# Column sums of the modulation products by one-column matmuls, and a shorter stage ahead of the first block, in a two-block transformer kernel

## The reference

```
mod = (silu(c) @ ada_w[l] + ada_b[l]).reshape(B, 3, 3, 1024)   # first block: 9 groups of 1024
h = rms_norm(x, norm_g[l, 0]) * (1 + scale) + shift
x = x + 0.5 * gate * swiglu(h, ffn1_w_in[l], ffn1_w_out[l])
ada = c_2 @ w_ada_2[l] + b_ada_2[l]                            # second block: 6 groups of 1024 per layer
```

## Time and profile before

| | us |
|---|---|
| median of 3 runs | 3195.17 |
| lowest, highest | 3194.53, 3200.88 |
| the profiled execution | 3195.94 |
| its span, first to last instruction | 3194.3 |
| TensorE, VectorE, ScalarE busy | 2939.4 (92%), 2336.1 (73%), 1363.4 (43%) |
| GpSimd busy | 186.3 (6%) |
| read from HBM | 545.29 MB, 171 GB/s over the span |
| mean granted TensorE clock | 0.956 of full |

### The profile page before, as it was taken

The page is one execution under the profiler, slowest core; times in us unless marked ns, Lnnn a source line. Parts: engine busy times, 40 slices in busy tenths (PEclk is TensorE's granted clock), DMA queues, the critical chain, the costliest instruction groups (busy, mean ns, idle before and its releaser), DMA issues.

```text
span 3194.3 us, 61745 instructions
## 1 busy us (share of the span) xinstructions
PE 2939.4 (92%) x22464; PEld 2718.6 (85%) x22464; DVE 2336.1 (73%) x3735; ACT 1363.4 (43%) x1973; POOL 186.3 (6%) x204
## 2 busy tenths in 40 slices
PE   3998997979989879999999999999799999999998
PEld 2998994969989778999998878898799899988787
DVE  6776933447778766997888986656449978899765
ACT  1434541224344524554444445445345544444444
POOL 1011000301101101011000000000000200000000
PEclk7999986989999989999999999999899999999999
DMA  7785530027867656444444545544345454445454
GB/s 274 273 276 169 180 133 14 1 92 245 276 211 282 199 178 224 159 163 159 163 158 152 165 156 191 195 153 137 102 154 175 152 165 158 160 156 170 159 194 140
DMA packets 149586, 547.98 MB, mean 172 GB/s; under 512 B 16609, under 2 KB 16737, under 8 KB 149089
## 3 DMA queue, kind: packets, MB, share of 16 engines
q1 hardware_dynamic: 124704, 454.29, 42.3%
q0 software_dynamic: 24336, 89.14, 8.4%
q10 hardware_dynamic: 432, 2.97, 0.2%
HBM read 545.29 MB, written 1.05 MB: 171 GB/s over the span
## 4 chain that ended last, share of the span: by engine, by line
PE 65%; DVE 11%; ACT 2%; issue 1%; DVEq 0%; ACTq 0%; POOL 0%; POOLq 0%
PE acc L1962 15%; PE st L1512 10%; PE st L1508 10%; PE st L1509 9%; PE acc L1968 7%; DVE w_lo L752 4%; PE st L1933 3%; PE acc L1508 2%; PE acc L1509 2%; PE acc L1512 2%; ACT w_hi L395 1%; DVE arena L1214 1%; PE st L1555 1%; PE acc L1891 1%; DVE arena L808 1%
## 5 line engine op out<-in xcount | busy, mean ns | idle before, releaser
L752 DVE TENSOR_TENSOR w_lo<-ring,w_hi 128x1024 fp32r<-128x1024 f32 x864 | 1087.3, 1260 | 553.1 <-ACT w_hi L395 545.8
L395 ACT ACTIVATE w_hi<-ring 128x1024 fp32r<-128x1024 f32 x864 | 910.6, 1054 | 1007.4 <-PE st L1512 821.0
L1508 PE MATMUL st<-h_hi,w_hi 128*128 128x256 f32 x3952 | 989.3, 288 | 6.1 <-ACT arena L681 3.5
L1509 PE MATMUL st<-h_lo,w_hi 128*128 128x256 f32 x3952 | 970.7, 283 | 0.0
L1508 PEld LDWEIGHTS st<-h_hi,w_hi 128*128 128x128 f32 x3952 | 758.2, 192 | 18.3 <-issue 9.7
L1509 PEld LDWEIGHTS st<-h_lo,w_hi 128*128 128x128 f32 x3952 | 759.2, 192 | 1.0
L1512 PE MATMUL st<-h_hi,w_lo 128*128 128x256 f32 x3952 | 559.1, 284 | 22.2 <-DVE w_lo L752 21.5
L1512 PEld LDWEIGHTS st<-h_hi,w_lo 128*128 128x128 f32 x3952 | 510.1, 192 | 29.8 <-DVE w_lo L752 29.6
L1962 PE MATMUL acc<-w_hi,act_hi 128*128 128x512 f32 x1016 | 322.5, 399 | 3.9 <-DVE act_lo L1326 3.9
L1962 PE MATMUL acc<-w_hi,act_lo 128*128 128x512 f32 x1016 | 316.0, 392 | 0.0
L714 ACT ACTIVATE act_hi<-arena 128x256 fp32r (+1 forms) x256 | 106.6, 418 | 409.4 <-PE acc L1968 401.2
(11 more groups left out here) (286 smaller groups left out, 3279.6 us busy)
## 6 DMA issues: line engine op xcount, KB each, us to landing
ring<-weights SPq DMA_DIRECT2D x864, 512.0 KB, 3.3
arena<-ada_weights POOLq DMA_DIRECT2D x168, 512.0 KB, 5.2
arena<-const ACTq DMA_DIRECT2D x1, 2112.0 KB, 8.7
x_t<-params SPq DMA_DIRECT2D x1, 1024.0 KB, 8.7
out<-arena POOLq DMA_DIRECT2D x1, 1024.0 KB, 4.2
k<-const ACTq DMA_DIRECT2D x1, 473.0 KB, 4.8
arena<-smallw ACTq DMA_DIRECT2D x1, 320.0 KB, 10.4
par<-params SPq DMA_DIRECT2D x1, 198.5 KB, 4.6
```

Source lines behind the costliest of these rows:

```text
L395: nc_a.activation(w_hi[:, u % 2, :], ring[:, u % RING, :], ACT.Copy).then_inc(hi_ready, 1)
L752: v.tensor_tensor(w_lo[:, u % 2, :], ring[:, u % RING, :], w_hi[:, u % 2, :], ALU.subtract)\
L1508: mm(dst(t), w, hi_t(t), start=start, stop=False, skip_group_check=True)
L1509: mm(dst(t), w, lo_t(t), start=False, stop=False, skip_group_check=True)
```

## The change

1. `piece` and `total` become `columns`: each of the eight 128x128 tiles of the summed buffer is the stationary operand, and one column of ones streams through it. The sums come out as a 128x8 column block in PSUM, in 8 matmuls per block.
2. `take` becomes one addition of the bias, PSUM to `mod` (128x8). The product with the identity, the reduction, `take_block`, `add_bias` and the buffer `diag` go.
3. `Q_FFN = (2, 8)`: only blocks 0 and 1 (shift and scale) are done in the stage "ada". Block 2 (the gate) moves into bodies 0 and 1 of the first feed-forward, block 3 into bodies 2 to 4: 4, 4, 3, 3, 2 macs. Before it was 0, 2, 2, 2, 2 (the second feed-forward keeps that).
4. `part_ffn` shrinks to two buffers; the first mac of a block in the loop waits until TensorE has read the buffer (`ada_piece`).
5. Transfers: x is issued when modulation unit 7 has landed, ring units 0 and 1 at unit 11, ring units 2 and 3 at unit 15.
6. ACT loads the silu table at once and squares x ahead of rounding units 0 and 1; DVE takes the reciprocal of the norm inside the stage, ahead of the stage's end.

```diff
@@ constants
-Q_FFN = (3, 8)
+Q_FFN = (2, 8)
+EARLY_MACS = (4, 4, 3, 3, 2)
+FIRST_IN_LOOP = (3, 8)
...
-        part_ffn = ar(4 * T, 5, UNIT)
+        part_ffn = ar(4 * T, 2, UNIT)
@@ SP
-            sp.wait_ge(ada_landed[1], 16)
+            sp.wait_ge(ada_landed[3], 32)
             sp.dma_start(x_t[:, :, :].rearrange("p a t -> p (a t)"), params[:, N_PAR:N_PAR + DT * T])\
               .then_inc(sem("x_in"), 16)
             for s in range(RING):
+                if s == 0:
+                    sp.wait_ge(ada_landed[3], 48)
+                elif s == 2:
+                    sp.wait_ge(ada_landed[3], 64)
                 sp.dma_start(ring[:, s, :], weights[s]).then_inc(landed[s], 16)
@@ ACT
+            eng.wait_ge(sem("zrow"), 1)
+            nc_a.activation(spare[:, :], spare[:, :], ACT.Silu)
             eng.wait_ge(sem("par_in"), 16)
             eng.wait_ge(sem("k1_in"), 16)
             nc_a.activation(sc[:, :], pc("c"), ACT.Silu).then_inc(sem("silu_c"), 1)
+            eng.wait_ge(sem("x_in"), 16)
+            squares(0)
             hi(U_FFN1)
             hi(U_FFN1 + 1)
-            eng.wait_ge(sem("x_in"), 16)
-            squares(0)
             stage(eng, ST["ada"])
@@ DVE
-            def take(q, r, src, i=None, upto=None, between=None):
...
-                v.tensor_tensor(diag, src.rearrange("p (u n) -> p u n", n=P),
-                                ident.unsqueeze(1).to_broadcast([P, 2, P]), ALU.mult).then_inc(ada_diag, 1)
...
-                v.tensor_reduce(dst, diag, AX, ALU.add).then_inc(sem("ada_mod"), 1)
...
+            def take(q, bank, i=None):
+                eng.wait_ge(ada_piece, plus(i, 1, q + 1))
...
+                v.tensor_tensor(dst, bank, bias, ALU.add).then_inc(sem("ada_mod"), 1)
...
                 for k in range(8):
                     mac(q, k, part[:, q % 2, :])
                     if k == 3 and q > 0:
-                        take_block(q - 1, st[:, 2 * ((q - 1) % 2):, :])
+                        take(q - 1, st[:, q - 1, 0:8])
+            eng.wait_ge(sem("x_in"), 16)
+            eng.wait_ge(sem("std"), 1)
+            link(v.reciprocal(rstd, std))
             lo(U_FFN1)
+            take(1, st[:, 1, 0:8])
+            taken_blocks(Q_FFN[0])
+            scale1_of(0)
             lo(U_FFN1 + 1)
-            take_block(Q_FFN[0] - 1, st[:, 2 * ((Q_FFN[0] - 1) % 2):, :])
-            add_bias(0, Q_FFN[0])
-            scale1_of(0)
...
                 def body(j, i=None, per=0):
                     t, k = max(j - 1, 0) // 4, (j - 1) % 4
+                    def macs(half):
+                        if j > 4:
+                            if (k, half) == (0, 0):
+                                eng.wait_ge(ada_piece, plus(i, 1, q0 + t))
+                            mac(q0 + t, 2 * k + half, part_ffn[:, 0, :], i)
+                        else:
+                            mine = early[j]
+                            for q, m in (mine[:len(mine) // 2], mine[len(mine) // 2:])[half]:
+                                mac(q, m, part_ffn[:, 1 if q < q0 else 0, :])
                     step(base + 2 + 3 * j, i, per)
+                    macs(0)
                     step(base + 3 + 3 * j, i, per)
                     mult(j + 1, i)
+                    if f == 0 and j == 4:
+                        take(q0 - 1, st[:, 2 + (j + 1) % 2, T:T + 8])
+                    if j > 4 and k == 0:
+                        take(q0 + t - 1, st[:, 2 + (j + 1) % 2, T:T + 8], i)
+                    macs(1)
+                    lower(j + 1, i)
+                    step(base + 4 + 3 * j, i, per)
...
-                take_block(q0 + 4, st[:, 2:4, :])
-                add_bias(q0, q0 + 5)
+                take(q0 + 4, st[:, 2, T:T + 8])
+                taken_blocks(q0 + 5)
@@ PE
-            def piece(q, r, dst, sums, i=None):
-                mm(dst, ones, sums, start=True, stop=True, skip_group_check=True).then_inc(ada_piece, 1)
...
+            def columns(q, dst, sums, i=None):
+                eng.wait_ge(ada_taken, plus(i, 8, 8 * q + 8))
+                for m in range(8):
+                    ins = mm(dst[:, m:m + 1], sums[:, m * P:(m + 1) * P], ones[:, 0:1], start=True, stop=True,
+                             skip_group_check=True)
+                ins.then_inc(ada_piece, 1)
...
-            for q in range(Q_FFN[0]):
-                total(q, st[:, 2 * (q % 2):, :], reused=q >= 2)
+            columns(0, st[:, 0, 0:8], part[:, 0, :])
             eng.wait_ge(sem("zrow"), 1)
             squares(0)
+            columns(1, st[:, 1, 0:8], part[:, 1, :])
             stage(eng, ST["ada"])
...
                 def body(j, i=None, per=0):
+                    if f == 0 and j == 4:
+                        columns(q0 - 1, st[:, 2 + (j + 1) % 2, T:T + 8], part_ffn[:, 1, :])
+                    if j > 4 and (j - 1) % 4 == 0:
+                        columns(q0 + (j - 1) // 4 - 1, st[:, 2 + (j + 1) % 2, T:T + 8], part_ffn[:, 0, :], i)
...
```

More of the change, by code:

```diff
@@ L121, with early_macs @@
 EXTRA = 3328
+FIRST_IN_LOOP = (3, 8)
+def early_macs(f):
+    if f == 0:
+        steps, counts = [(q, m) for q in (2, 3) for m in range(8)], EARLY_MACS
+    else:
+        steps, counts = [(Q_FFN[1], m) for m in range(8)], (0, 2, 2, 2, 2)
+    ends = [sum(counts[:j + 1]) for j in range(5)]
+    return [steps[e - c:e] for e, c in zip(ends, counts)]
 def build(nc, weights, ada_weights, params, const1, const2, smallw, out):
@@ L746, in _ @@
             v = nc.vector
+            v.memset(spare[:, :], 0.0)
             v.memset(zrow[:, :], 0.0).then_inc(sem("zrow"), 1)
@@ L810, in mac, with taken_blocks @@
                 ins.then_inc(ada_taken, 1)
[L812 to L835 removed]
+            def take(q, bank, i=None):
+                eng.wait_ge(ada_piece, plus(i, 1, q + 1))
+                at = _COLS["ada_b"][0] + 8 * q
+                dst, bias = (mod[:, 8 * q:8 * q + 8], par[:, at:at + 8]) if i is None else \
+                    (mod[:, bass.ds(i * 8 + 8 * q, 8)], par[:, bass.ds(i * 8 + at, 8)])
+                v.tensor_tensor(dst, bank, bias, ALU.add).then_inc(sem("ada_mod"), 1)
+            def taken_blocks(n):
+                eng.wait_ge(sem("ada_mod"), n)
             def scale1_of(s):
@@ L1146, in _ @@
                 if l == 0:
-                    take_block(Q_PROJ + 2, st[:, 0:2, :])
+                    take(Q_PROJ + 2, st[:, 0, 0:8])
                 for m in range(2):
@@ L1163, in out_steps @@
                             if k in OUT_TAKES:
-                                q = OUT_TAKES[k]
-                                take_block(q, banks[:, 2 * (q % 2):, :])
+                                take(OUT_TAKES[k], banks[:, 3, 0:8])
                 out_steps(0, 4)
@@ L1621, in ffn @@
                 eng.wait_ge(sem("act_lo"), FT * f + FT)
-                for r in range(4):
-                    piece(q0 + 4, r, quarter(st[:, 2:4, :], r), part_ffn[:, 4, r * T:(r + 1) * T])
+                columns(q0 + 4, st[:, 2, T:T + 8], part_ffn[:, 0, :])
                 b = (FT - 1) % 2
@@ L1860, in _ @@
                     eng.wait_ge(sem("smax"), AH)
-                    total(Q_PROJ + 2, st[:, 0:2, :])
+                    columns(Q_PROJ + 2, st[:, 0, 0:8], part[:, (Q_PROJ + 2) % 2, :])
                 stage(eng, ST[f"attn{l}"])
@@ L1866, in behind_out @@
                         q = OUT_TAKES[k + 1]
-                        total(q, banks[:, 2 * (q % 2):, :])
+                        columns(q, banks[:, 3, 0:8], part[:, q % 2, :])
                 kmajor(U + O_AP, 4, behind=behind_out)
@@ L1895, in _ @@
                 if l == 0:
-                    total(N_BLOCKS - 1, st[:, 2:4, :])
+                    columns(N_BLOCKS - 1, st[:, 3, 0:8], part[:, (N_BLOCKS - 1) % 2, :])
                 base = U + O_PEER
```

65 lines of the change are left out of this document (13 added, 52 removed).

## The result

| | before | after |
|---|---|---|
| median of the runs of this comparison | 3196.28 (4) | 3174.80 (4) |
| lowest, highest | 3194.53, 3200.88 | 3162.85, 3176.25 |
| the profiled execution, its span | 3195.94, 3194.3 | 3174.65, 3173.0 |
| mean granted TensorE clock | 0.956 | 0.954 |

The ratio is 0.9924, with a 95% interval of 0.9912 to 0.9935. The change makes the kernel faster by 21 us, half of what I forecast, and 3174.8 lies outside my range of 3143 to 3168.

The account below looks back on a forecast made before the run. Waits of TensorE, behind modulation transfers and VectorE's takes, were what the change could shrink. 27.9 - 4.0 + 1.0 + 6.8 + 10.3 = 42.0 us from the profiled 3195.94 gave 3153.9, forecast 3153; range 3143 to 3168.

Parts of the forecast that it names:

- x hides: First stage: x, issued near 19, is expected to land in 5 us and have its root taken by 36.5.
- The first bodies: First feed-forward, bodies 0 to 4: moved macs 1.0, block 2's columns 1.8, transfer waits 1.2; together 4.0 us lost.
- The second block: Each take falls from 3.74 to 0.2 us, so TensorE waits less; 10.3 us gained, bounds 4 and 15.
- (b): Second block, block 15 in front of the stage's end, where TensorE waits 5.84 us: 3.0 us gained.
- (c): Second block, block 16 ahead of the merge on which the 8.51 us wait hangs: 2.5 us gained.
- (a): Second block, blocks 13, 14, 17, 18, 19: TensorE's 0.86 us wait for `w_lo` behind each goes; 4.3 us gained.
- (d): Second block, block 20 ahead of the top-16 search: 0.5 us gained, taken from between 0 and 3.5.
- The first stage: Modulation stage: 16 macs instead of 24, last mac ends at 36.5, norm starts at 41.4 instead of 69.33; 27.9 us gained.
- rival of fast transfers: First stage: slots return at 3.6 us, 1.35 us per unit, byte bound 31.4 holds; 5 us more, 3148; chance 0.17.
- The ends of the feed-forwards: Behind the last body: one addition readies the gate near 278.0, then banks set the pace; 3.4 us each, 6.8 gained.
- The loops: Both feed-forward loops: shorter waits give 1.0 us per feed-forward, columns against pieces lose 0.5; 1.0 us gained in both.
- The rival of the clock: First bodies: TensorE stays at 1.2 GHz; over five bodies the whole gain is gone, over ten 3240 us; chance 0.03.

Follow-up runs that it names:

- e8: e2 with 16 places of their own for the first 16 modulation units, all issued at once; 3143.60 us, ratio 0.9830.
- e7: e2 with the eight matmuls behind the last body of both feed-forwards streaming 128 columns each in place of one; 3147.92 us, ratio 0.9845.
- e3: The changed kernel with 32 streaming columns of ones in place of one in both feed-forwards; 3160.37 us, ratio 0.9878.
- e4: The changed kernel with the sums inside both feed-forward loops made as before (256-column pieces, identity products, reductions); 3164.56 us, ratio 0.9894.
- e2: The changed kernel with the columns in both feed-forward loops moved from the body's start to between its first two units; 3151.33 us, ratio 0.9854.

## Why the prediction was wrong, point by point

Of the 20.7 us that are missing, 13.9 are in the two feed-forwards: there my sum let every matmul behind a group of columns run at the full clock, and it did not. 3.5 are the rate of the modulation units in the first stage. 5.6 are in the mixer, whose code is the same; 2.9 of them are left in the means of three profiles each. The second block gave 2.4 more than forecast.

**Right.** The first mac (7.33, forecast 7.2). The silu table gave nothing. x hides: issued at 19.0, landed in 8.9 us, its root was taken at 34.1, ahead of the last mac. From the last mac to the first norm operation 5.4 us, of which 0.74 are a wait for columns at half clock; forecast 4.9. The first bodies: to the end of body 4 TensorE needed 55.96 us against 50.95 before, so 5.0 lost, forecast 4.0; the two waits for `w_lo` are 0.48 and 0.49, the columns 1.8. A term that I had not counted is the clock: from the first matmul on the half level lasts 5.8 us (46.96 to about 52.8) where it was 3.0 before (71.15 to about 74.1), some 1.4 us of work. That is the rival I had named, in small. The wait of VectorE on `ada_piece` cost nothing. A block's columns cost 1.8 us at full clock, as read from the 16-column rows.

**The second block, near by luck in part.** It gave 12.7, forecast 10.3. At (b) 1.9 us less waiting, where I had 3.0; at (c) 2.65, where I had 2.5. The waits of (a) are all gone, but the trace of before has four of them (at 1004.62, 1030.49, 1182.92 and 1250.10), not five: 3.4 us, not 4.3. Of (d) nothing shows: behind the reciprocal at 1201.8 the block gained 1.0, which the wait at 1250.10 nearly accounts for. These make 8.0; the other 4.7 had no term of mine. The clock is in it: the squares ahead of that reciprocal took 5.41 us before and 3.72 after.

**The first stage, a term mis-sized.** I took a unit per 1.85 us, from the median landing of before, 5.8 us, and said of it that it "has the collisions of before in it". The collisions did not go; the median landing in the stage became 6.4. The same formula with it, (6.4 + 1.28 + 0.5) / 4 = 2.05 us, gives 7.3 + 15 x 2.05 + 1.3 = 39.4, and the last mac ended at 39.5. The slots as the limit were right, and e8 shows it: without them the last mac ended at 32.0. Of the page's rule (the Trainium skill, DMA: Bandwidth & Descriptors, Anatomy of one DMA), by which a landing is near 3.2 us, an estimate, no modulation unit of the kernel after shows even the value: the shortest landing is 4.6 in the stage and 3.4 in the whole run. My rival of fast transfers at 31.4 us came true only in e8, where nothing waits for a slot.

**The ends of the feed-forwards, the step that failed.** "then the banks set the pace, the last at 280.2" assumed 2.88 us for TensorE's last unit, that is, the full clock. The unit ran at half speed behind thin columns and a wait of 1.46 us. 0.7 of 3.4 was left. The mechanism was right: e7 changes only the width of these matmuls and gets 9.00 us in place of 12.77, 3.8 gained.

**The loops, the same failure.** I wrote that of columns against pieces "Nearly nothing comes from TensorE". From the end of body 4 to the columns behind the last body it is 156.67 us after and 153.45 before: 3.2 lost instead of 0.5 gained. As in the term before, each column group was priced at 1.8 us and the matmuls behind it at the full clock. In three profiles the falls make PEclk 0.96 or 0.91 in ten of the twelve windows of the loop.

**The rival of the clock had the wrong place.** I named a clock that stays low over the first bodies, priced it at the whole gain or more, and gave it 0.03. I argued that "waits of tenths are no idle stretch". What came was not one long stay but short falls of 3.4 us, about 1.7 us each, behind waits of 1.1 to 1.5 us, in places that I had gone through only for their duration. The waits were in my own rows: 1.49 us ahead of a piece, with no fall behind it. What I did not ask was what the work next to this wait does with the clock when it gets thinner. In each feed-forward of the kernel after there are three such falls in the loop and one at the end that lasts as long as the last unit (PEclk 0.52 over the 7 us from 261, and again over the 6.8 us from 926.8):

```profile
261.00:268.00 7.00, 7.00 (x32) 6.88 (x33) 3.57 (x10) 2.52 (x7) 0.00 (x0) 0.52 0.23 76
926.80:933.60 6.80, 6.80 (x31) 6.68 (x32) 3.64 (x10) 2.58 (x7) 0.00 (x0) 0.52 0.25 78
```

That is 3 x 1.7 + 3.4 = 8.5 us of TensorE's work for each, 17 for both, where 13.9 are missing in the two feed-forwards. Before, each end had a fall too, 1.7 us (PEclk 0.57 from 282 to 286 and from 941 to 945); less these the sum is 13.6. It is an estimate, and leaves out the 1.0 us of the first bodies.

**The range** had no room for it, since my own forecast's terms all assumed the full clock. Had I let each of the ten column groups in the feed-forwards cost one fall, 1.7 us, the clock's case would have stood at 3153 + 17 = 3170, and with 3 us more for the stage at 3173, next to the 3174.8 measured, and not at 3195 or more.

## What to carry to other kernels

When a change makes the work next to a TensorE wait thinner, price what the clock does there, not only the instructions: here the same eight matmuls cost 1.8 us between two units, and about 1.1 of waiting and 1.7 of half speed more at a body's start. Put small work of TensorE between full matmuls, behind which its input has long been ready; where a wait can't be avoided, let the matmuls stream more columns (128 cost no more than one in e7). And where a stream's landing time was read while its ring was full, count its rate by slots with the landing that the new kernel will have, or give it more slots: 16 places instead of 4 gave 6 us.

## What the runs showed that I had not expected

Eight float32 matmuls of one column and eight of 128 columns both take 1.81 us to the next matmul at full clock (0.23 each): up to that width the stream is not what is paid for.

The runs of one kernel differ along with their mean granted clock: the four of the kernel after are 3162.85 us at a mean granted clock of 0.957, and 3174.65 to 3176.25 at 0.954 and 0.953. A difference of 0.4% in the clock is 13 us of 3174, so a single profile pair can tell a stage only to a few microseconds; the mixer of before, 435.8 to 440.8 in three profiles, shows it within one stage.

In e3 and e4 TensorE waited in the loop as long as after (4.3 us) or longer (5.7), and the clock fell once in eight passes or not at all. It is thus neither the wait alone nor the thin matmuls alone (e2) that brought it down here, but both side by side.
